# Value products of a head in column halves of the array, all six together, and VectorE's order in a head

## What is computed

```python
def one_block(qblk):
    s = jnp.einsum('bqhd,bkhd->bhqk', qblk, k).astype(F32) * scale
    p = jax.nn.softmax(s, axis=-1).astype(v.dtype)
    return jnp.einsum('bhqk,bkhd->bqhd', p, v)
...
ox = block_attention(qx, jnp.concatenate([kc, kx], axis=1), jnp.concatenate([vc, vx], axis=1))
x = x + g1 * (ox @ mla_w_o[j])
```

## Time and profile before

| | |
|---|---|
| median of 3 executions | 1861.57 us (1856.65 to 1864.16) |
| profiled execution | 1861.37 us, span 1859.3 us |
| mean granted TensorE clock | 0.982 of full speed |
| TensorE busy | 1791.2 us, 96% of the span |
| GpSimd busy | 1076.8 us, 58% |
| VectorE busy | 1039.7 us, 56% |
| ScalarE busy | 520.5 us, 28% |
| value products (line 2146) | 192 passes, 100.9 us busy |
| normalisation on GpSimd (line 1834) | 64 instructions, 174.8 us busy |
| modulation rows (line 2671) | 80 instructions, 97.2 us busy |

### The profile page before, as it was taken

How to read it: one execution, slowest core, us unless ns; L and a number is a source line. 1 busy time by engine, 2 the same in 40 slices (tenths; PEclk the granted TensorE clock), 3 DMA queues, 4 the chain that set the end, 5 groups by cost and what they waited for, 6 DMA issues and landing times.

```text
span 1859.3 us, 23742 instructions
## 1 busy us (share of the span) xinstructions
PE 1791.2 (96%) x8526; PEld 1409.6 (76%) x8526; DVE 1039.7 (56%) x1482; ACT 520.5 (28%) x923; POOL 1076.8 (58%) x699
## 2 busy tenths in 40 slices
PE   8989999999999999999999998999999999999998
PEld 1765655558888887778787887888888888777886
DVE  5647666666775443344467736666438338627173
ACT  2444444442432323211222214322222121113111
POOL 1447776755566666555566344666666634446663
PEclk9999999999999999999999998999999989999998
DMA  8215555632233433333422222343333333223332
GB/s 332 60 62 175 171 193 159 189 111 80 74 102 102 136 102 123 108 134 133 148 91 91 68 68 75 101 137 113 100 109 121 111 143 129 69 60 94 91 101 81
DMA packets 55370, 216.00 MB, mean 116 GB/s; under 512 B 6145, under 2 KB 8321, under 8 KB 52610
## 3 DMA queue, kind: packets, MB, share of 16 engines
q1 hardware_dynamic: 50834, 201.31, 33.6%
q10 hardware_dynamic: 4464, 13.70, 1.9%
HBM read 200.83 MB, written 14.16 MB: 116 GB/s over the span
## 4 chain that ended last, share of the span: by engine, by line
PE 86%; POOL 6%; DVE 4%; issue 1%; ACT 1%; DMA 1%; DVEq 0%; SPq 0%; POOLq 0%; ACTq 0%
PE PS L1877 24%; PE PS L1879 23%; PE PS L1878 23%; POOL PR L1834 5%; PE PS L2124 2%; PE PS L2146 2%; PE PS L2009 2%; PE PS L2136 2%; PE PS L718 1%; PE PS L1378 1%; PE PS L2125 1%; POOL WL L1819 1%; PE PS L1362 1%; PE PS L507 1%; DVE PS L2834 1%
## 5 line engine op out<-in xcount | busy, mean ns | idle before, releaser
L1819 POOL TENSOR_TENSOR WL<-RAW,WH 128x1024 fp32r<-128x1024 f32 (+3 forms) x238 | 607.7, 2553 | 19.9
L1877 PE MATMUL PS<-HH,WH 128*128 128x512 f32 (+1 forms) x1416 | 546.5, 386 | 27.2 <-POOL WL L1819 13.2
L1878 PE MATMUL PS<-HL,WH 128*128 128x512 f32 (+1 forms) x1416 | 539.0, 381 | 0.0
L1879 PE MATMUL PS<-HH,WL 128*128 128x512 f32 (+1 forms) x1416 | 538.6, 380 | 0.0
L1816 POOL TENSOR_SCALAR WH<-RAW 128x1024 fp32r<-128x1024 f32 (+3 forms) x238 | 266.8, 1121 | 294.7 <-PE PS L1879 260.4
L1877 PEld LDWEIGHTS PS<-HH,WH 128*128 128x128 f32 x1416 | 270.6, 191 | 86.5 <-issue 17.6
L1879 PEld LDWEIGHTS PS<-HH,WL 128*128 128x128 f32 x1416 | 270.8, 191 | 49.9
L1878 PEld LDWEIGHTS PS<-HL,WH 128*128 128x128 f32 x1416 | 271.2, 192 | 48.6 <-issue 0.2
L1815 POOL TENSOR_TENSOR SC<-ONES 1x1 f32<-1x1 f32 x146 | 31.2, 214 | 362.3 <-PE PS L1879 348.6
L1834 POOL TENSOR_SCALAR PR<-PR,SC 128x768 f32<-128x768 f32 x64 | 174.8, 2746 | 83.0 <-DVE SC L2701 83.0
L1877 PE MATMUL PS<-HIDH,WH 128*128 128x512 f32 (+1 forms) x396 | 149.1, 377 | 0.0
(11 more groups left out here) (401 smaller groups left out, 2558.0 us busy)
## 6 DMA issues: line engine op xcount, KB each, us to landing
RAW<-in_wup SPq DMA_DIRECT2D x88, 512.0 KB, 3.5
MR<-in_modw SPq DMA_DIRECT2D x80, 512.0 KB, 3.6
RAW<-in_wdn SPq DMA_DIRECT2D x32, 704.0 KB, 4.1
RAW<-in_whin SPq DMA_DIRECT2D x28, 512.0 KB, 3.6
RAW<-in_whead SPq DMA_DIRECT2D x8, 640.0 KB, 4.3
MK<-in_modk SPq DMA_DIRECT2D x4, 1024.0 KB, 16.1
MK<-in_modk SPq DMA_DIRECT2D x2, 2048.0 KB, 16.4
RAW<-in_wo SPq DMA_DIRECT2D x8, 512.0 KB, 3.8
```

Source lines behind the costliest of these rows:

```text
L1819: pool.tensor_tensor(WL[s][:, 0:n], RAW[s][:, 0:n], WH[s][:, 0:n].bitcast(F32), ALU.subtract).then_inc(tile_split, 1)
L1877: pe.matmul(out, wh, xh, start=first, stop=False)
L1878: pe.matmul(out, wh, xl, start=False, stop=False)
L1879: return pe.matmul(out, wl, xh, start=False, stop=last)
```

## The change

The value product of a head no longer uses both heads' columns. Its weights are the 64 columns of this head; the queries 0 to 255 go through columns 0 to 63 of the array and end in PSUM partitions 0 to 63, the queries 256 to 511 through columns 64 to 127 into partitions 64 to 127, both in the first 256 places of the bank. Each key tile thus has two products of 256 queries in place of one of 512. All twelve stand together at the end of the head, behind the transposes, the query projection of h+2 and, in even heads, the keys of the next pair, which now come after the query. The wait for the weight tile moves from the keys to the query, and the keys wait for all six copies of turned probabilities, whose PSUM banks they use. The output's high and low parts are written in two instructions of 256 queries. ScalarE copies the keys before the output. VectorE makes row 0 before the first maximum, then all four maxima, and row 1, row 2, the scaled queries, row 3, the value copy (now in even heads, one pair ahead), rows 4 and 5, and the low part of the output last.

```diff
@@ project_keys
-                pe.wait_ge(tile_split, i * per + (t + 1))
@@ project_query
                 if h >= 2:
-                    pe.wait_ge(S["olo"], i * per + (h - 2))
+                    if h % 2 == 0:
+                        pe.wait_ge(tile_split, i * (per // 2) + (t + 1))
+                    pe.wait_ge(S["olo"], i * (2 * per) + (2 * h - 4))
@@
-            def value(h, kt, i=0, per=0):
-
-                if kt == 0:
-                    pe.wait_ge(S["vc"], i * (per // 2) + (h // 2 + 1))
-                    pe.wait_ge(S["qready"], i * per + min(h + 2, 16))
-                pe.wait_ge(S["pt"], i * (6 * per) + (6 * h + kt + 1) + 1)
-                m = pe.matmul(bank(4 + h % 2), VC[h // 2 % 2][:, kt, :], PT[:, kt, :], start=kt == 0, stop=kt == 5)
-                if kt == 5:
-                    m.then_inc(S["pv"], 1)
+            def value(h, i=0, per=0):
+
+                pe.wait_ge(S["vc"], i * (per // 2) + (h // 2 + 1))
+                pe.wait_ge(S["qready"], i * per + min(h + 2, 16))
+                pe.wait_ge(S["pt"], i * (6 * per) + (6 * h + 6) + 1)
+                v = slice(VH * (h % 2), VH * (h % 2) + VH)
+                for kt in range(6):
+                    for half in range(2):
+                        m = pe.matmul(PS[VH * half:VH * half + VH, 4 + h % 2, 0:256], VC[h // 2 % 2][:, kt, v],
+                                      PT[:, kt, tok(half)], start=kt == 0, stop=kt == 5)
+                m.then_inc(S["pv"], 1)
@@ head, tensor
                     if h < 15:
                         score(h + 1, qt, i, per)
-                    value(h, qt, i, per)
-                    if qt < 3:
-                        turn(h, qt + 2, i, per)
-                    else:
-                        turn(h, 5, i, per)
-                value(h, 4, i, per)
-                value(h, 5, i, per)
+                    turn(h, qt + 2, i, per)
                 if h < 14:
+                    project_query(h + 2, i, per)
                     if h % 2 == 0:
+                        pe.wait_ge(S["pt"], i * (6 * per) + (6 * h + 6) + 1)
                         project_keys(h // 2 + 1, i, per // 2)
-                    project_query(h + 2, i, per)
+                value(h, i, per)
@@ out_hi, scalar (out_lo on VectorE likewise)
-                act.copy(HH[v, ds(i * (per // 2) + h // 2, 1), :].rearrange("p a n -> p (a n)"),
-                         PS[v, 4 + h % 2, :]).then_inc(S["ohi"], 1)
+                for half in range(2):
+                    act.copy(HH[v, ds(i * (per // 2) + h // 2, 1), tok(half)].rearrange("p a n -> p (a n)"),
+                             PS[VH * half:VH * half + VH, 4 + h % 2, 0:256]).then_inc(S["ohi"], 1)
@@ head, scalar
                 if h < 14 and h % 2 == 0:
-                    out_hi(h, i, per)
                     keys(h // 2 + 1, i, per // 2)
-                else:
-                    out_hi(h, i, per)
+                out_hi(h, i, per)
@@ value_copy, vector
-                if p >= 2:
+                if p:
@@ head, vector
+                row(0)
                 if h < 15:
                     maximum(h + 1, 0, i, per)
-                    row(0)
                     for qt in range(1, 4):
                         maximum(h + 1, qt, i, per)
                         inverse_sum(h + 1, qt - 1, i, per)
-                        row(qt)
+                    row(1)
                     inverse_sum(h + 1, 3, i, per)
-                if h % 2 == 1 and h < 13:
-                    value_copy(h // 2 + 2, i, per // 2)
-                row(4)
-                out_lo(h, i, per)
-                row(5)
+                row(2)
                 if h < 14:
                     query(h + 2, i, per)
+                row(3)
+                if h % 2 == 0 and h < 14:
+                    value_copy(h // 2 + 1, i, per // 2)
+                row(4)
+                row(5)
+                out_lo(h, i, per)
```

More of the change, by code:

```diff
@@ L1900, in linear @@
                         if heads:
-                            pe.wait_ge(S["olo"], 2 * k + 2)
+                            pe.wait_ge(S["olo"], 4 * k + 4)
                         if ready is not None:
@@ L2347, in keys @@
                     else:
-                        act.wait_ge(S["proj"], i * (3 * per) + (3 * p + 1 + c if p else 3))
+                        act.wait_ge(S["proj"], i * (3 * per) + (3 * p + 2 + c if p else 3))
                     for hb in range(2):
@@ L2685, in query @@
                 else:
-                    dve.wait_ge(S["proj"], i * (3 * per // 2) + (3 * (h // 2) + 3))
+                    dve.wait_ge(S["proj"], i * (3 * per // 2) + (3 * (h // 2) + 1))
                 dve.tensor_tensor(Q[h % 2][:, :], bank(4 + (h + 1) % 2), QTAB[:, :], ALU.mult
@@ L2711, in out_lo @@
                 v = slice(VH * (h % 2), VH * (h % 2) + VH)
-                at = (v, ds(i * (per // 2) + h // 2, 1), slice(None))
-                dve.wait_ge(S["ohi"], i * per + (h + 1))
-                dve.tensor_tensor(HL[at].rearrange("p a n -> p (a n)"), PS[v, 4 + h % 2, :],
-                                  HH[at].rearrange("p a n -> p (a n)").bitcast(F32),
-                                  ALU.subtract).then_inc(S["olo"], 1)
+                for half in range(2):
+                    at = (v, ds(i * (per // 2) + h // 2, 1), tok(half))
+                    dve.wait_ge(S["ohi"], i * (2 * per) + (2 * h + half + 1))
+                    dve.tensor_tensor(HL[at].rearrange("p a n -> p (a n)"), PS[VH * half:VH * half + VH, 4 + h % 2, 0:256],
+                                      HH[at].rearrange("p a n -> p (a n)").bitcast(F32),
+                                      ALU.subtract).then_inc(S["olo"], 1)
             def head(h, rows, i=0, per=0):
@@ L2755, in _ @@
             value_copy(0)
-            value_copy(1)
             with repeat(dve, 3) as i:
```

## The result

The changed kernel takes 1908.0 us (median of 4 runs, 1905.66 to 1912.79) against 1860.3 us for the kernel before: ratio 1.0259, 95% interval 1.023 to 1.0289. The forecast was 1867 us with a range of 1842 to 1877, so the time lies 41 us above the forecast and outside the range. The profiled execution has a span of 1906.8 us, against 1859.3 before.

What follows compares the result with a forecast made beforehand. VectorE's loop of row loads on two buffers was to set each pair of heads, 36.46 us against 36.77. From 1861.37 us, -1.6 us in all and +7.2 for clock falls gave 1867 us, range 1842 to 1877.

Steps and rivals of the forecast that it cites:

- The bound: Attention heads: VectorE waiting for row loads on two buffers replaces GpSimd and TensorE, 36.46 us a pair against 36.77.
- first maximum to row 1: VectorE's four maxima close up with no row between, paced by scores, transposes and exponential: 6.2 us in each head.
- row 1 to row 3: Row 3 needs row 1's buffer refilled: one buffer turn of 4.9 us in each head.
- row 5 to the next row 0: Even head's end on VectorE: row 5 at 1.22 us, then out_lo as two halves at 0.8 us.
- the sum: VectorE's loop per pair of heads: 19.24 us even plus 17.22 us odd, 36.46 us against 36.77 now.
- The clock: TensorE's idle stretches in a pair lower its granted clock: 1.2 us a pair, bounds 0 and 2.5.
- mostly covered: Clock fall after TensorE's second gap, 3.4 us idle behind the odd head's value products; the maximum can wait 0.4 to 0.9 us.
- rival 4: Attention heads: loads return soon enough, GpSimd's 33.6 us set the pair; 1840 us, halfway 1850; chance 15%.
- The landing: Modulation row loads: 3.5 us to landing in the row taken; all 80 in 3.3 to 5.6 us, median 3.6.
- The value products: Head's end on TensorE: 24 passes of 256 columns, the two halves side by side, 2.6 us.
- Rival 5: Value products: each column-tiled pass waits for its load or the array to empty; 1890 us at v = 8; chance 10%.
- rival 3: Value products: the halves run one after the other, 5.2 us, and the clock holds; 1860 us; chance 18%.

Runs made afterwards that it cites:

- e1: The changed kernel with VectorE's rows 0 to 3 put back between the maxima, as in the kernel before: 1845.68 us.
- e2: The kernel before with only VectorE's new order and its value copy; value products stay full width between the scores: 1947.76 us.
- e4: The changed kernel with 78 of the 80 modulation row loads left out, rows working on what their buffers hold: 1861.21 us.
- e6: The changed kernel with TensorE's query projection of head h+2 moved from behind the last transposes to ahead of score 2: 1889.52 us.
- e9: The changed kernel with the query projection ahead of score 2 and GpSimd's weight split ahead of the odd head's normalisation: 1878.75 us.
- e10: The changed kernel with e8's row order in even heads; in odd heads row 0 follows maximum 1, the others one place later: 1833.08 us.
- e8: The changed kernel with rows spread: row 0 ahead of the first maximum, rows 1 to 3 behind maxima 1 to 3: 1845.38 us.
- e5: The changed kernel with full-width value products again (128 columns, 512 queries, six a head), still together at the head's end: 1916.87 us.

## Why the prediction was wrong

**The bound: right.** Loads, two buffers and the maxima take the place of GpSimd and TensorE, link by link as the prediction lists them; e1, e2 and e4 show it. The sizes were wrong. The links, means over the six pairs of the changed kernel, beside the prediction's terms:

| link of VectorE's loop, us | even head, predicted | measured | odd head, predicted | measured |
|---|---|---|---|---|
| first maximum to row 1 | 6.2 | 8.12 | 6.2 | 8.20 |
| row 1 to row 3 | 4.9 | 4.92 | 4.9 | 4.96 |
| row 3 to row 5 (odd: to the next row 0) | 4.9 | 6.40 | 4.9 | 5.84 |
| row 5 to the next row 0 | 2.02 | 3.76 | | |
| row 0 to first maximum | 1.22 | 1.27 | 1.22 | 1.27 |
| sum | 19.24 | 24.47 | 17.22 | 20.27 |

The pair was put at 36.46 us, and 37.66 with the clock; it measures 44.7. Three terms make the difference, and the second is the step that failed outright: the sum had no wait for it.

**The clock: mis-sized.** The prediction took 1.2 us a pair, with bounds of 0 and 2.5. Measured are 1.9 + 2.0 = 3.9 us on the two links with the maxima. The prediction had one gap ahead of score 2, in odd heads, and a second that the maxima wouldn't feel ("mostly covered"). In fact the gap stands ahead of score 2 in every head, 5.6 us on average, because the loop is longer than the sum had it; both falls hit scores 2 and 3, straight on the loop. e6 confirms 3.1 us of the term: with part of the gap filled the links are 6.32 and 6.88.

**GpSimd's lock: missing.** From row 3 to the next head's row 0 the even head takes 10.16 us instead of 6.92, 3.2 us a pair, and no term stood for it. The prediction moved row 4 and the value copy later without asking what GpSimd runs at that moment. It had both times: the split fills the gap between GpSimd's two normalisations, and rows 3 to 5 now come in the same stretch. A row was taken at 1.22 us from a profile in which hardly one meets the split (80 rows, 97.2 us in all; 124.4 in the profile after). e9's undisturbed pairs and e10 confirm the term. The lock also works the other way and stood in the profile before: a normalisation takes 2.20 us alone, but 2.73 us on average there, because most of them begin during a row. The four of 10.6 and 11.8 us, on which rival 4 rests, hold 1.8 and 3.0 us of such waits.

**The landing: a little off.** In odd heads row 3 to the next row 0 takes 5.84 instead of 4.9 us, +0.9 a pair. This link has the next weight tile's load on the same queue ahead of it: the row loads issued next behind a weight tile's landed after 3.9 to 5.1 us, the others after 3.7 in the middle. The prediction allowed it up to 1 us, but for a row "with 0.9 us of slack", and there is none. That the weight tile makes the 0.9 us is read from these loads; no run took it away alone. Over all the changed kernel's row loads between 174 and 444 us the landings are those of the earlier trace rows:

```profile
DMA to landing us min/median/max: 3.4/3.7/5.1
```

Together 3.9 + 3.2 + 0.9 = 8.0 of the 8.3 us by which the pair exceeds the sum's 36.46. The six pairs make 6 x (44.9 - 37.66) = 43 us of the miss. Their start and heads 14 and 15, where the sum saved 2.2 us, cost 4.0, which is 6 more. So the stage is 49 us above its sum; the forecast was only 41 short because the rest of the kernel came out 7 us shorter, which no term had foreseen. That part is chance.

**The value products: right.** 2.6 us taken, 2.81 measured for the 24 passes. The Trainium skill, TensorE: Matmul & The Clock Gate, Part 3, led to an estimate of 3.2 us; the trace lies below it. The Trainium skill, TensorEngine Tiling (Array Packing), Key Properties, says that the change of mode drains the engine. From the last key pass ahead of the block (193.12) to the first transposition behind it (196.07) it is 2.95 us; one step of the keys (0.12) and twelve of the block (0.215 each) make 2.70, so 0.25 us is left for both changes of mode. Rival 5's cause wasn't there, and rival 3's neither.

**The signs that were named.** Row 3 waits for DMA: yes, 1.36 us instead of 1.7; row 5 doesn't, as its load came while row 4 stood still, and the next row 0 waits 1.90. Even heads of 16 and odd ones of 20 us: no, 21.8 and 23.1. GpSimd released by VectorE: yes. Score 2 idle on ScalarE: yes, but in every head and longer. Clock about 0.9: 0.87. Value passes 0.11 us apart: yes on average, 2.81 us for 24; the two halves of a key tile start under 0.01 us apart, and the next tile's 0.21 us later. GpSimd's start at 5.47 us after the head's start shows only where VectorE's loop is out of the way, as 5.28 in e10.

**The range.** Terms that feed one another were added as if they stood apart: the lock lengthens the loop, the loop lengthens the gap, the gap the time at low clock, and that the maxima, which are on the loop. The range took each one's own bound and nothing for their chain.

## What to carry to other kernels

Before an instruction with two inputs in SBUF (the on-chip memory of the engines) is moved on VectorE, look up what GpSimd runs at its new place: price it at the rest of that instruction plus its own time, unless the trace shows such a pair side by side. Look at single instructions for that, since a mean over a group hides the collision. Uses of two buffers that are refilled after each use belong spread over the stage: the same rows bunched behind the maxima cost 62 us against the same kernel with them spread. Where a new bound makes idle stretches on TensorE, put what follows them at half clock on the path, and lengthen the loop by it, before the range is set.

## What the runs showed of the hardware

A row of VectorE (two inputs) that begins while GpSimd's L1819 (two inputs) runs makes no headway until that ends. It ends 1.08 us after it in the changed kernel and in e4, and 1.09 in e8, whether it began 0.5 us (196.54, 197.04) or 1.7 us (188.80, 190.51) into it, and takes up to 3.9 us instead of 1.22. L1816, the split's first instruction, has one input and does the same. In e8 the row ends at 189.79, 1.07 us after it:

```profile
187.46 1.26 POOL L1816 TENSOR_SCALAR WH<-RAW 128x1280 fp32r<-128x1280 f32 x1
188.01 1.77 DVE L2669 CUSTOM_DVE_ANT_0 MR<-MR,CB 128x1024 f32<-128x1024 f32 x1 [2.60 <-DMA MR<-in_modw]
```

It works the other way too: a GpSimd instruction that begins during a row waits for the row. A normalisation (L1834) takes 2.20 us alone. This one of the changed kernel began during the row of 189.09 to 190.30 and ends 2.07 us after it:

```profile
189.30 3.07 POOL L1834 TENSOR_SCALAR PR<-PR,SC 128x768 f32<-128x768 f32 x1
```

Over all 13 traces, 367 normalisations began during a row, and they end 2.07 us after it (one 2.24). The Trainium skill, SBUF — State Buffer, Who interferes with whom, says that a VectorE instruction with two SBUF inputs and a GpSimd instruction that reads SBUF exclude each other, the later one for the whole length of the first; these rows agree. One combination doesn't: a row that begins during a normalisation isn't held to its end. The row at 190.30, right behind the one that had held the normalisation, takes 1.84 us and ends before it, and rows that begin 0.9 us or more into a normalisation's own 2.20 us take 1.20 to 1.25, as alone. There the measurement decides.

Products with weights for 64 columns, one in each half of the array, run side by side at full rate: 24 passes of 256 queries in 2.81 us at clock 1.00, about half of the 5.32 us of e5's twelve full passes of 512, also at clock 1.00.

After 4 us in which TensorE had no work at clock 1.00, the next 4 us were granted 0.57, a mixture of its two levels, 2.4 and 1.2 GHz. In the longer idle stretch of 6.8 us the clock fell within it (0.70), and the 4.2 us of scores behind it ran at 1.2 GHz throughout (0.50).
